# A decoder layer on one core: the convolution tiles cut into three passes, pages loaded from another queue, and three waits refilled or moved

## The chip, the cores and the metric

The kernel runs on one core of a Trainium2 chip. The metric is device time in microseconds (us), median of several runs; smaller is better. TensorE does the matrix products, VectorE (DVE in the rows), ScalarE (ACT) and GpSimd (POOL) the rest, and SyncE (SP) issues most transfers.

## The reference

One layer of inference for 256 prompt tokens and 8 sequences of 4 sample tokens, so 288 columns in all, with d_model 1024:

```
mod = silu(c) @ w_ada + b_ada            # shift1, scale1, gate1, shift2, scale2, gate2
h   = rms_norm(x) * (1 + scale1) + shift1
q, k, v, qi, ki, wi, u_conv, gates = split(h @ w_in)
A = sparse_attention(top 64 or 65 keys by the indexer, ALiBi softmax) @ w_o_attn
B = silu(layer_norm(causal_conv31(a * sigmoid(g)) + b_dw)) @ w_conv_out   # a, g = halves of u_conv
x = x + gate1 * ((sigmoid(gA) * A + sigmoid(gB) * B) @ w_out)
h2 = rms_norm(x) * (1 + scale2) + shift2
# PEER: top 16 of 16384 experts per head, gelu(u_emb . h2) * softmax gate, times v_emb
x = x + gate2 * peer(h2)
```

## The kernel before

All weights come as tiles of 128 x 1024 fp32 (512 KB) through a ring of four buffers, loaded by SP in the order of PLAN; the load of tile n waits until tile n-4 has been used. A linear tile is 8 products of 128 x 128 weights with 288 columns. It is computed in one of two ways. `linear` uses fp32 operands as they are (TensorE takes them in a slow mode). `linear_cut` cuts weights and activations into a high and a low fp32r part and makes three passes of 8 products: high x high, high x low, low x high. The high part of a tile is a copy on ScalarE (`cut_tile`), its low part a subtraction on GpSimd (`low_tile`); two cut buffers alternate. CUT lists the tiles done that way.

HEAD is the first stretch. It holds, per channel chunk k of 128, the tile conv_a k, the tile conv_g k and a part of the adaLN product (`ada`, 4 fp32 products per half, 32 columns wide); then ki, the four qi tiles, v, the k and q tiles. ScalarE applies the sigmoid to conv_g k, VectorE multiplies it with conv_a k (`gated_input`) and makes the 31-tap convolution of chunk k as 31 dependent multiply-adds of 128 x 256 on a PSUM accumulator. `settle(n)` makes VectorE wait until all but its last n recorded steps are complete; `conv_a k` for k >= 3 waits until chunk k-3 is gated. In HEAD ScalarE also issues the loads of the 16 cache pages (`load_page`), two with each conv_g tile. After the convolution VectorE does the sample tokens (a product and a reduction of 128 x 1984 for each of the four), sums the chunks for the LayerNorm, takes the reciprocal of the q/k norms, and then feeds the indexer, whose loop of 16 steps alternates on TensorE with the gate_a tiles. `L1947` is the product that spreads the q/k norms.

The second norm follows the eight out tiles: TensorE sums the squares (L1736), ScalarE and VectorE turn them into h2, and TensorE meanwhile makes one of the two last adaLN groups (`late_ada`, L1840) and then peer_q 0, with the other group between its products. After the 16 peer_q tiles the score tiles begin (128 of them, `scores`), each with a high cut on ScalarE (`cut_high`), a low cut on GpSimd (`cut_low`) and a gelu on ScalarE. At score tile 16 (SOFTMAX) ScalarE makes three exponentials for the expert gates. All engines run their own program in order, and wait on semaphores.

Of the kernel before, what the change touches and what calls it, by code (L numbers as in the profile page):

```python
# [18 lines left out]
P = 128  # L19
D = 1024  # L20
KC = D // P
# [19 lines left out]
R = 4  # L41
# [123 lines left out]
QK_AT = 3  # L165

# [10 lines left out]
def build(nc, a):  # L177
# [4 lines left out]
    with ExitStack() as ctx:  # L182
# [33 lines left out]
        class Region:  # L216
# [101 lines left out]
        windows = xn[:, :, :].rearrange("p k t -> p (k t)")[:, 0:KC * NSEQ * CW]\  # L318
            .rearrange("p (k b j) -> p k b j", b=NSEQ, j=CW)
# [77 lines left out]
        late_loaded = [sem(f"late_loaded{n}") for n in range(2 * R)]  # L397
# [43 lines left out]
        conv_in = sem("conv_in")  # L441
        vw_in = sem("vw_in")
# [93 lines left out]
        def _(sp):  # L536
            def load(n, slot):
                sp.dma_start(ring[:, slot, :], a["stream"][n]).then_inc(tile_loaded[slot], 16)

            for n, at in enumerate(LOADS):  # L540
# [5 lines left out]
                load(at, n % R)  # L546
                late = n - POS["attn_out", 2]
# [76 lines left out]
        def _(pool):  # L624
# [32 lines left out]

            for n in range(NHEAD - 2):
                low_tile(n)

# [3 lines left out]
            for n in range(NHEAD - 2, NHEAD):  # L664
                low_tile(n)
            low_tiles(("gate_a",))
# [23 lines left out]
            pool.wait_ge(tile_done, NRING)  # L690
# [10 lines left out]
            for n in range(R):  # L701
                cut_low(n, n, u_done, n - 1 if n >= 2 else None)
# [36 lines left out]
        def _(eng):  # L739
# [25 lines left out]
            for dst, src in ((staged_s, "stateT"), (wdw, "wdw"), (cvec, "cvec"), (qkg, "qkg")):  # L765
                eng.dma_start(dst, a[src]).then_inc(conv_in, 16)
# [41 lines left out]
            def load_page(n):  # L808
                page = eng.value_load(pages[0:1, n:n + 1], min_val=0, max_val=a["cache_k"].shape[0] - 1)
                for dst, src in ((cache_i[0:ID, n], "cache_i"), (cache_i[ID:P, n], "cache_i"),  # L810
                                 (cache_k[:, n].rearrange("p v n -> p (v n)"), "cache_k"), (cache_v[:, n], "cache_v")):
                    eng.dma_start(dst, a[src][bass.ds(page, 1)].rearrange("o p n -> (o p) n")).then_inc(cache_in, 16)

            for key in HEAD:
# [15 lines left out]
                elif kind == "conv_g":  # L830
                    eng.wait_ge(tile_done, POS[key] + 1)
                    nc.scalar.activation(sig[:, m], lin[BANK[key]][:, 0:T], ACT.Sigmoid).then_inc(sig_ready, 1)

                    eng.wait_ge(pages_in, 16)
                    for n in (2 * m, 2 * m + 1):
                        load_page(n)
# [140 lines left out]

            eng.wait_ge(stored, 16 * 4)
            for n in range(2 * PH):
                if n + 1 < 2 * PH:  # L980
                    cut_tile(("peer_q", n + 1))
                evac(("peer_q", n), qh[:, n])
# [21 lines left out]
            def cut_high(c, n, loaded, first=False):  # L1004

                eng.wait_ge(tile_loaded[slot_of(n)], loaded)
                if not first:

                    eng.wait_ge(hi_used, c - 1)
                    eng.wait_ge(lo_ready, c - 1)  # L1010
                nc.scalar.activation(split[:, n % 2, 0], ring[:, slot_of(n), :], ACT.Copy).then_inc(hi_ready, 1)  # L1011

# [8 lines left out]
            def first_of(n):  # L1021
                return 16 * (loads_before(n) + 1)


            eng.wait_ge(x_stored, 16)
            eng.wait_ge(tile_done, NRING)
            cut_high(0, 0, first_of(0), True)
# [4 lines left out]
            def turn(g, tokens4):  # L1032

                for n in range(R):
# [5 lines left out]
                    nc.scalar.activation(act[:, n % 2], ps[n % 2][:, 0:T], ACT.Gelu_apprx_tanh).then_inc(gelued, 1)  # L1040
                    if tokens4:
# [5 lines left out]

            with eng.Fori(1, SOFTMAX // R) as g:
# [42 lines left out]
        def _(dve):  # L1091
# [63 lines left out]
            dve.wait_ge(conv_in, 64)  # L1155
            dve.wait_ge(state_in, 1)
            dve.wait_ge(zeroed, 6)
            def gated_input(pair):
                for k in (2 * pair, 2 * pair + 1):
# [8 lines left out]
            gated_input(0)  # L1168
            for pair in range(KC // 2):
                dve.wait_ge(z_ready, 4 * pair + 4)  # L1170
                if pair:
                    dve.wait_ge(y_prompt, 2 * pair)
                for j in range(CW):
                    if j == (CW // 2 if pair == 0 else CW // 4) and pair + 1 < KC // 2:
                        gated_input(pair + 1)
                    for k in (2 * pair, 2 * pair + 1):
# [3 lines left out]
                        else:  # L1180

                            settle(1 if j < CW - 1 or k % 2 == 0 else 0)
# [7 lines left out]

            samples = y[:, :, TP:T].rearrange("p k (b t) -> p k b t", t=TD)
            dve.wait_ge(y_prompt, KC)
            step(V.tensor_copy(wdw_ps, wdw))
# [536 lines left out]
        def _(pe):  # L1730
# [7 lines left out]

            def linear(key, rhs, chunk_ready=None):

                if key[0] == "conv_a":
                    bank = pa[key[1] % 3]
                    if key[1] >= 3:

# [581 lines left out]
```

## Time and profile before

| what | value |
|---|---|
| median of 3 runs | 1259.42 us (1259.25 to 1259.59) |
| profiled execution, own time | 1258.07 us |
| its span | 1256.2 us |
| PE busy | 1213.9 us, 97% |
| DVE busy | 923.6 us, 74% |
| ACT busy | 584.4 us, 47% |
| POOL busy | 571.7 us, 46% |
| mean DMA rate | 217 GB/s |

The span is the stretch from the first to the last instruction of the profiled execution; its own time is 1.9 us longer. The busy shares are means over stages with different limits. Times in rows are counted from the start of the span.

### The profile page before, as it was taken

The numbers are of one execution on the slowest core, as the hardware profiler recorded it, in microseconds if no ns is written. First come the engines' busy times: TensorE is split into PE (matmuls) and PEld (weight loads), VectorE is DVE, ScalarE is ACT, GpSimd is POOL, SyncE is SP. The second block draws the span as 40 slices with busy tenths as digits, with TensorE's granted clock in tenths as the row PEclk, the third lists the DMA queues.
The fourth block names the chain that finished last, engine by engine and source line by source line (L and its number), as shares of the span: only waits on it lengthen the run. The fifth ranks groups of instructions, "written<-read, shape, count | busy, mean of one in ns | idle before, by whom it ended". The sixth has DMA issues, their size and how long they took to land.

```text
span 1256.2 us, 27868 instructions
## 1 busy us (share of the span) xinstructions
PE 1213.9 (97%) x8703; PEld 1110.1 (88%) x8703; DVE 923.6 (74%) x2247; ACT 584.4 (47%) x1005; POOL 571.7 (46%) x286
## 2 busy tenths in 40 slices
PE   5999999989989999999999999999999999999997
PEld 3777887989979999999999999999888888888886
DVE  4499985966754999959999999000467888888866
ACT  2202355657533445545555555444445554555453
POOL 0203454521755566766666666777303334343100
PEclk9999999999989999999999999999999999999999
DMA  9876465423743355665555555667767898888863
GB/s 361 312 266 209 150 225 188 141 85 123 264 143 123 130 185 192 203 204 176 188 178 185 179 185 179 211 210 233 252 239 272 311 342 295 312 304 307 276 230 128
DMA packets 113996, 273.11 MB, mean 217 GB/s; under 512 B 30929, under 2 KB 54193, under 8 KB 113553
## 3 DMA queue, kind: packets, MB, share of 16 engines
q1 hardware_dynamic: 98752, 243.71, 56.6%
q0 software_dynamic: 6432, 19.71, 4.6%
q10 hardware_dynamic: 8752, 8.93, 2.1%
q8 instruction: 33, 0.54, 0.2%
q14 instruction: 27, 0.21, 0.1%
HBM read 249.30 MB, written 23.00 MB: 217 GB/s over the span
## 4 chain that ended last, share of the span: by engine, by line
PE 90%; DVE 2%; DMA 2%; issue 2%; POOL 1%; ACT 1%; SPq 1%; ACTq 0%; DVEq 0%; POOLq 0%
PE ps L2185 19%; PE ps L2135 10%; PE ps L2128 10%; PE ps L2129 10%; PE ps L2188 10%; PE ps L1797 6%; PE ps L1813 6%; PE ps L1807 5%; PE ps L1755 5%; PE ps L2164 2%; DMA ring<-in_stream 1%; PE ps L1829 1%; POOL split L698 1%; PE ps L1901 1%; PE ps L2105 1%
## 5 line engine op out<-in xcount | busy, mean ns | idle before, releaser
L698 POOL TENSOR_TENSOR split<-ring,split 128x1024 fp32r<-128x1024 f32 x128 | 307.2, 2402 | 142.8 <-ACT split L1011 140.2
L1011 ACT ACTIVATE split<-ring 128x1024 fp32r<-128x1024 f32 x256 | 271.5, 1061 | 175.6 <-PE ps L2185 167.1
L2128 PE MATMUL ps<-h2r,split 128*128 128x288 f32 x1024 | 278.8, 297 | 3.2 <-ACT split L1011 3.1
L2129 PE MATMUL ps<-h2r,split 128*128 128x288 f32 x1024 | 279.0, 296 | 0.0
L2185 PE MATMUL ps<-h2r,split 128*128 128x512 f32 x1024 | 257.4, 392 | 1.4 <-DVE h2r L1644 1.4
L649 POOL TENSOR_TENSOR split<-ring,split 128x1024 fp32r<-128x1024 f32 x62 | 151.9, 2452 | 234.0 <-ACT split L796 228.0
L2185 PEld LDWEIGHTS ps<-h2r,split 128*128 128x128 f32 x1024 | 184.2, 189 | 34.5 <-ACT act L1040 1.6
L2128 PEld LDWEIGHTS ps<-h2r,split 128*128 128x128 f32 x1024 | 192.9, 188 | 3.9 <-issue 2.1
L2129 PEld LDWEIGHTS ps<-h2r,split 128*128 128x128 f32 x1024 | 192.6, 188 | 0.0
L2135 PE MATMUL ps<-h2r,split 128*128 128x288 f32 x1024 | 156.9, 295 | 0.3
L1650 DVE TENSOR_TENSOR split<-ring,split 128x1024 fp32r<-128x1024 f32 x128 | 156.0, 1218 | 0.0
L1040 ACT ACTIVATE act<-ps 128x288 f32<-128x288 f32 x124 | 51.0, 412 | 213.2 <-PE ps L2135 209.2
L2188 PEld LDWEIGHTS ps<-h2r,split 128*128 128x128 f32 x1024 | 140.1, 190 | 9.9
L2188 PE MATMUL ps<-h2r,split 128*128 128x256 f32 x1024 | 143.8, 282 | 0.0
L2135 PEld LDWEIGHTS ps<-h2r,split 128*128 128x128 f32 x1024 | 141.4, 188 | 1.5 <-POOL split L698 1.5
L711 POOL DMA_INDIRECT big<-in_stream,pick_at x32 | 58.2, 1820 | 180.1 <-DVE big L1664 132.7
L1603 DVE SCALAR_TENSOR_TENSOR hot<-ps,parts 128x256 fp32r<-128x256 f32 x256 | 124.0, 484 | 0.0
L1602 DVE TENSOR_SCALAR hot<-ps,parts 128x128 fp32r<-128x128 f32 x256 | 89.8, 351 | 11.2 <-PE ps L2164 11.2
L1183 DVE SCALAR_TENSOR_TENSOR ps<-big,ps 128x256 f32<-128x256 f32 x232 | 91.5, 480 | 0.0
L1638 DVE TENSOR_TENSOR parts<-parts,big 128x256 f32<-128x256 f32 x64 | 27.1, 424 | 82.0 <-DMA parts<-act_dram 82.0
L796 ACT ACTIVATE split<-ring 128x1024 fp32r<-128x1024 f32 x70 | 73.8, 1055 | 25.0 <-DMA ring<-in_stream 14.3
L1797 PE MATMUL ps<-h2r,split 128*128 128x288 f32 x432 | 73.0, 309 | 5.4 <-issue 2.7
(286 smaller groups left out, 1687.4 us busy)
## 6 DMA issues: line engine op xcount, KB each, us to landing
ring<-in_stream SPq DMA_DIRECT2D x371, 512.0 KB, 3.5
act_dram<-act SPq DMA_DIRECT2D x128, 128.0 KB, 1.7
big<-in_stream SPq DMA_DIRECT2D x20, 512.0 KB, 7.4
parts<-act_dram SPq DMA_DIRECT2D x16, 512.0 KB, 4.7
big<-act_dram SPq DMA_DIRECT2D x16, 512.0 KB, 5.6
big<-in_cache_k ACTq DMA_DIRECT2D x16, 128.0 KB, 3.4
big<-in_cache_v ACTq DMA_DIRECT2D x16, 128.0 KB, 3.3
s_act_dram<-act SPq DMA_DIRECT2D x128, 16.0 KB, 1.5
```

Source lines behind the costliest of these rows:

```text
L649: nc.gpsimd.tensor_tensor(split[:, n % 2, 1], ring[:, POS[CUT[n]] % R, :], split[:, n % 2, 0].bitcast(f32), ALU.subtract).then_inc(lin_lo, 1)
L698: nc.gpsimd.tensor_tensor(split[:, n % 2, 1], ring[:, slot_of(n), :], split[:, n % 2, 0].bitcast(f32), ALU.subtract).then_inc(lo_ready, 1)
L1011: nc.scalar.activation(split[:, n % 2, 0], ring[:, slot_of(n), :], ACT.Copy).then_inc(hi_ready, 1)
L1183: ins = V.scalar_tensor_tensor(acc if j < CW - 1 else y[:, k, 0:TP], zp[:, k, j:j + TP], w, acc, ALU.mult, ALU.add)
L1603: return V.scalar_tensor_tensor(hot1[:, slot], iota_ps.unsqueeze(1).to_broadcast([P, 2, P]), parts[:, 0, col], parts[:, 2:4, col].to_broad ...
L1650: V.tensor_tensor(split[:, n % 2, 1], ring[:, slot_of(n), :], split[:, n % 2, 0].bitcast(f32), ALU.subtract).then_inc(lo_ready, 1)
L1797: MM(out, hi[:, k], rhs_h[:, k], start=(k == 0), stop=False)
L2128: MM(out, u_hi[:, k], h_hi[:, k], start=(k == 0), stop=False)
L2129: last = MM(out, u_hi[:, k], h_lo[:, k], start=False, stop=False)
L2135: last = MM(out, u_lo[:, k], h_hi[:, k], start=False, stop=(k == KC - 1))
L2185: return MM(ps[k][:, 0:2 * TP], v[0][:, k], w_both, start=first, stop=last)
L2188: return MM(ps[k][:, 0:TP], v[1][:, k], wr[:, n % 2, 0], start=False, stop=False)
```

## The change

The front. The convolution tiles, but for chunk 0, join CUT. The pages are issued by SP, one behind each second tile load from position 20 on. VectorE takes the convolution chunks as 0, (1, 2), (3, 4), (5, 6), 7 and waits for the taps only, which are now loaded before the convolution state. The sum of the prompt's chunks goes to GpSimd, and the bias of the sample tokens becomes a 32nd element of the reduced window.

The back. TensorE makes products that nobody reads (`keep_busy`) at the second norm, 6 and then 2 behind each `late_ada`. The first score tile is cut before the last peer_q tile is evacuated. The exponentials stand behind the first gelu of a turn of four that is written out, outside the loop.

```diff
-STAGES = [("qi", "k", "q", "gate_a", "gate_b"), ("conv_out",), ("attn_out",), ("out",), ("peer_q",)]
-CUT = [key for key in PLAN if any(key[0] in kinds for kinds in STAGES)]
+STAGES = [("conv_a", "conv_g", "qi", "k", "q", "gate_a", "gate_b"), ("conv_out",), ("attn_out",), ("out",), ("peer_q",)]
+CUT = [key for key in PLAN if any(key[0] in kinds for kinds in STAGES) and key not in (("conv_a", 0), ("conv_g", 0))]
+GROUPS = [(0,)] + [(k, k + 1) for k in range(1, KC - 1, 2)] + [(KC - 1,)]
+PAGE_POS = NFIRST * R + R
...
                 load(at, n % R)
+                page, odd = divmod(n - PAGE_POS, 2)
+                if 0 <= page < NSEQ * NPAGES and not odd:
+                    sp.wait_ge(pages_in, 16)
+                    load_page(page)
...
+            def add_chunk(k):
+
+                pool.wait_ge(y_prompt, k + 1)
+                if k > 1:
+                    pool.wait_ge(prompt_sum, k - 1)
+                nc.gpsimd.tensor_tensor(over_y[:, 0:TP], y[:, 0, 0:TP] if k == 1 else over_y[:, 0:TP], y[:, k, 0:TP], ALU.add)\
+                    .then_inc(prompt_sum, 1)
+
             for n in range(NHEAD - 2):
                 low_tile(n)
+                for k in {15: (1, 2), 20: (3, 4), 25: (5, 6)}.get(n, ()):
+                    add_chunk(k)
...
-            pool.wait_ge(tile_done, NRING)
+            pool.wait_ge(tile_done, NRING - 1)
...
-            eng.wait_ge(conv_in, 64)
-            nc.scalar.activation(zs[:, :, :, 0:LEFT], staged_s, ACT.Copy).then_inc(state_in, 1)
+            nc.scalar.activation(warm, eps, ACT.Sigmoid)
...
-            gated_input(0)
-            for pair in range(KC // 2):
-                dve.wait_ge(z_ready, 4 * pair + 4)
-                if pair:
-                    dve.wait_ge(y_prompt, 2 * pair)
+            gated_input(GROUPS[0])
+            for g, group in enumerate(GROUPS):
+                dve.wait_ge(z_ready, 2 * group[-1] + 2)
+                if g:
+
+                    dve.wait_ge(y_prompt, group[0])
                 for j in range(CW):
-                    if j == (CW // 2 if pair == 0 else CW // 4) and pair + 1 < KC // 2:
-                        gated_input(pair + 1)
-                    for k in (2 * pair, 2 * pair + 1):
+                    if j == (CW - 1 if g == 0 else CW // 4) and g + 1 < len(GROUPS):
+                        gated_input(GROUPS[g + 1])
+                    for i, k in enumerate(group):
...
-                            settle(1 if j < CW - 1 or k % 2 == 0 else 0)
+                            settle(len(group) - 1 if j < CW - 1 or i == 0 else 0)
...
+            def keep_busy(n):
+
+                for _ in range(n):
+                    MM(pa[3][:, 0:T], g_lo[:, 0, 0:P], g_lo[:, 0], start=True, stop=True)
+
+            keep_busy(6)
             pe.wait_ge(chunk_sums, 4)
             pe.wait_ge(squares2, KC)
             sums(y[:, 0], y[:, KC - 1])
@@
             for s in range(R):
                 for j in range(2):
                     late_ada(0, s, j)
+                    keep_busy(2)
...
             with eng.Fori(1, SOFTMAX // R) as g:
                 turn(g, False)
-
-            for t in range(NT):
-                eng.wait_ge(top_max, t + 1)
-                nc.scalar.activation(tv[:, t, 0:HEADS[t]], tv[:, t, 0:HEADS[t]], ACT.Exp).then_inc(top_exp, 1)
-            with eng.Fori(SOFTMAX // R, TURN // R) as g:
+            turn(SOFTMAX // R, False, exponentials)
+            with eng.Fori(SOFTMAX // R + 1, TURN // R) as g:
                 turn(g, False)
```

On ScalarE, the front of HEAD of the kernel before: the state copy (L806), the sigmoid of conv_g (L832) and the page loads (L809, L812) between the sigmoids.

```order
L801 ACTIVATE h2r<-big 128x288 x8
L806 ACTIVATE big<-big 128x64x30
L832 ACT_TABLE_LOAD
L832 ACTIVATE big<-ps 128x288
L809 TENSOR_LOAD pages
L809 ISA x2
L812 ISA
L812 DMA big<-in_cache_i 64x128 x2
```

The same place of the changed kernel, where L837 is the warm-up sigmoid, L857 the sigmoid of conv_g and L828 the high cut of a tile.

```order
L833 ACTIVATE h2r<-big 128x288 x8
L837 ACT_TABLE_LOAD
L837 ACTIVATE big<-big 128x1
L828 ACTIVATE split<-ring 128x1024
L857 ACTIVATE big<-ps 128x288
L828 ACTIVATE split<-ring 128x1024 x2
L857 ACTIVATE big<-ps 128x288
```

The state copy and the pages are gone from here, and two cuts now stand ahead of each sigmoid: the second of them is the cut of the next chunk's conv_a tile.

On TensorE, the second norm of the kernel before: the sum of squares (L1736), the late adaLN group (L1840) and the start of peer_q 0 (L1797).

```order
L1736 MATMUL ps<-big,ones 128x288 x2
L1840 MATMUL ps<-big 32x128 x32
L1797 MATMUL ps<-h2r,split 128x288
L1840 MATMUL ps<-big 32x128 x4
L1797 MATMUL ps<-h2r,split 128x288
```

The same place of the changed kernel, where L2120 are the products that nobody reads, L1770 the sum of squares and L1875 the adaLN group.

```order
L2120 MATMUL ps<-y_r 128x288 x6
L1770 MATMUL ps<-big,ones 128x288 x2
L1875 MATMUL ps<-big 32x128 x4
L2120 MATMUL ps<-y_r 128x288 x2
L1875 MATMUL ps<-big 32x128 x4
L2120 MATMUL ps<-y_r 128x288 x2
```

The group of 32 products is now broken into 8 pieces of 4, each followed by 2 of the new products, 22 of them in all with the first 6.

On ScalarE, the exponentials (L1053) of the kernel before, and the loop of score tiles behind them with its cuts (L1011) and gelus (L1040).

```order
L1053 ACT_TABLE_LOAD
L1053 ACTIVATE big<-big 128x128 x2
L1053 ACTIVATE big<-big 128x32
L1054 UNCONDITIONAL_BRANCH
L1054 ISA
L1009 REGISTER_ALU
L1011 ACT_TABLE_LOAD
L1011 ACTIVATE split<-ring 128x1024
L1037 REGISTER_ALU
L1039 REGISTER_ALU
L1040 ACT_TABLE_LOAD
L1040 ACTIVATE act<-ps 128x288
```

The same place of the changed kernel, where L1009 is the cut, L1065 the gelu and L1078 the exponentials.

```order
L1009 ACTIVATE split<-ring 128x1024
L1065 ACTIVATE act<-ps 128x288
L1078 ACT_TABLE_LOAD
L1078 ACTIVATE big<-big 128x128 x2
L1078 ACTIVATE big<-big 128x32
L1009 ACTIVATE split<-ring 128x1024
L1065 ACT_TABLE_LOAD
L1065 ACTIVATE act<-ps 128x288
L1009 ACTIVATE split<-ring 128x1024
```

The exponentials stand one cut and one gelu later, one table load stands between them and the next gelu, and no table load stands in a loop any more; before, the loop of three turns held two.

## Rows read from the trace of the kernel before

**Rows 1.** The page's part 4, shares of the chain that ended last, by engine.

```profile
PE 90%; DVE 2%; DMA 2%; issue 2%; POOL 1%; ACT 1%; SPq 1%; ACTq 0%; DVEq 0%; POOLq 0%
```

**Rows 2.** Windows: busy us (x instructions) of PE, PEld, DVE, ACT, POOL; clock; DMA share; GB/s.

```profile
40.00:60.00 20.00, 20.00 (x109) 15.03 (x108) 10.51 (x28) 4.33 (x5) 0.00 (x0) 1.00 0.85 295
371.00:373.00 2.00, 2.00 (x19) 0.89 (x18) 2.00 (x6) 1.11 (x2) 0.81 (x1) 0.50 0.00 0
```

**Rows 3.** Timeline of TensorE in the front: start, length, instruction, [idle before].

```profile
38.48 8.03 PE L1755 MATMUL ps<-big,ring 128*128 128x288 f32 x32
...
98.31 4.15 PE L1755 MATMUL ps<-big,ring 128*128 128x288 f32 x16
...
107.58 1.32 PE L1813 MATMUL ps<-h2r,split 128*128 128x288 f32 x8
...
109.41 1.32 PE L1797 MATMUL ps<-h2r,split 128*128 128x288 f32 x8
...
112.71 1.23 PE L1797 MATMUL ps<-h2r,split 128*128 128x288 f32 x8
```

**Rows 4.** Timeline of VectorE: the convolution, the sample tokens, the q/k reciprocal.

```profile
77.28 0.99 DVE L1179 TENSOR_SCALAR ps<-big 128x256 f32<-128x256 f32 x2
...
102.73 0.99 DVE L1179 TENSOR_SCALAR ps<-big 128x256 f32<-128x256 f32 x2
...
152.70 0.42 DVE L1193 COPY ps<-big 128x248 f32<-128x248 f32 x1
153.15 2.22 DVE L1196 TENSOR_TENSOR big<-big,ps 128x1984 f32<-128x1984 f32 x1
...
179.50 1.94 DVE L1208 RECIPROCAL big<-big 10x288 f32<-10x288 f32 x1 [1.93 <-ACT big L859]
```

**Rows 5.** One line, L1183: the multiply-add of the convolution, ns min/median/max.

```profile
L1183 DVE SCALAR_TENSOR_TENSOR ps<-big,ps x232: 475/481/484, 51.4 to 151.4; 128x256 f32<-128x256 f32 x116
```

**Rows 6.** Timeline of TensorE: the product that spreads the q/k norms.

```profile
182.50 0.75 PE L1947 MATMUL ps<-big,ident 10*128 10x288 f32 x2
```

**Rows 7.** Timelines of GpSimd: low part of the activations; low part of a tile.

```profile
34.41 5.17 POOL L640 TENSOR_TENSOR h2r<-big,h2r 128x2304 fp32r<-128x2304 f32 x1 [1.87 <-ACT h2r L801]
...
110.38 2.40 POOL L649 TENSOR_TENSOR split<-ring,split 128x1024 fp32r<-128x1024 f32 x1 [0.50 <-ACT split L796]
```

**Rows 8.** Timeline of ScalarE's queue: first issues of two pages in a row.

```profile
50.52 1.14 ACTq L812 DMA_DIRECT2D big<-in_cache_i  x2
...
53.52 0.49 ACTq L812 DMA_DIRECT2D big<-in_cache_i  x1
```

**Rows 9.** DMA issues from 25 to 110 us: count, KB each, median us to landing.

```profile
ring<-in_stream SPq DMA_DIRECT2D x31, 512.0 KB, 4.9
```

**Rows 10.** Timeline of TensorE at the second norm.

```profile
363.92 1.95 PE L1840 MATMUL ps<-big 128*32 128x128 f32 x64
368.52 0.37 PE L1797 MATMUL ps<-h2r,split 128*128 128x288 f32 x1 [2.64 <-ACT h2r L975]
...
369.18 0.40 PE L1797 MATMUL ps<-h2r,split 128*128 128x288 f32 x1
...
380.18 1.47 PE L1797 MATMUL ps<-h2r,split 128*128 128x288 f32 x8
```

**Rows 11.** Timelines of TensorE and ScalarE: first score tile, and third passes of score tiles.

```profile
441.83 0.38 ACT L1000 ACTIVATE big<-ps 128x256 f32<-128x256 f32 x1
...
443.30 0.37 PE L2128 MATMUL ps<-h2r,split 128*128 128x288 f32 x1 [1.53 <-ACT split L1011]
...
445.77 1.34 PE L2135 MATMUL ps<-h2r,split 128*128 128x288 f32 x8
...
497.09 1.23 PE L2135 MATMUL ps<-h2r,split 128*128 128x288 f32 x8
...
531.88 1.23 PE L2135 MATMUL ps<-h2r,split 128*128 128x288 f32 x8
```

**Rows 12.** Timeline of ScalarE around the exponentials.

```profile
495.59 1.28 ACT L1053 ACT_TABLE_LOAD   x1
...
497.53 1.28 ACT L1011 ACT_TABLE_LOAD   x1
498.82 1.06 ACT L1011 ACTIVATE split<-ring 128x1024 fp32r<-128x1024 f32 x1
```

More of the change, by code:

```diff
@@ L396, in build @@
         wide_loaded = [sem(f"wide_loaded{n}") for n in range(NWIDE)]
-        late_loaded = [sem(f"late_loaded{n}") for n in range(2 * R)]
+        late_loaded = wide_loaded[0:2 * R]
         late_done = sem("late_done")
@@ L538, in load, with load_page @@
                 sp.dma_start(ring[:, slot, :], a["stream"][n]).then_inc(tile_loaded[slot], 16)
+            def load_page(n):
+                page = sp.value_load(pages[0:1, n:n + 1], min_val=0, max_val=a["cache_k"].shape[0] - 1)
+                for dst, src in ((cache_i[0:ID, n], "cache_i"), (cache_i[ID:P, n], "cache_i"),
+                                 (cache_k[:, n].rearrange("p v n -> p (v n)"), "cache_k"), (cache_v[:, n], "cache_v")):
+                    sp.dma_start(dst, a[src][bass.ds(page, 1)].rearrange("o p n -> (o p) n")).then_inc(cache_in, 16)
             for n, at in enumerate(LOADS):
@@ L976, in _, with cut_high, first_of @@
                     .then_inc(rhs_hi, 1)
+            def cut_high(c, n, loaded, first=False):
+                eng.wait_ge(tile_loaded[slot_of(n)], loaded)
+                if not first:
+                    eng.wait_ge(hi_used, c - 1)
+                    eng.wait_ge(lo_ready, c - 1)
+                nc.scalar.activation(split[:, n % 2, 0], ring[:, slot_of(n), :], ACT.Copy).then_inc(hi_ready, 1)
+            def first_of(n):
+                return 16 * (loads_before(n) + 1)
             eng.wait_ge(stored, 16 * 4)
@@ L981, in _ @@
                     cut_tile(("peer_q", n + 1))
+                else:
+                    eng.wait_ge(x_stored, 16)
+                    eng.wait_ge(tile_done, NRING - 1)
+                    cut_high(0, 0, first_of(0), True)
                 evac(("peer_q", n), qh[:, n])
@@ L1030, in _, with turn @@
                 gelu(c, c, c < 2)
-            def turn(g, tokens4):
+            def turn(g, tokens4, behind_first=None):
                 for n in range(R):
@@ L1040, in turn @@
                     nc.scalar.activation(act[:, n % 2], ps[n % 2][:, 0:T], ACT.Gelu_apprx_tanh).then_inc(gelued, 1)
+                    if behind_first and n == 0:
+                        behind_first()
                     if tokens4:
@@ L1153, in _, with gated_input @@
                     V.tensor_tensor(smp, smp, wide(mod[:, 0, k, 1:NG]), ALU.add).then_inc(h_ready, 1)
-            dve.wait_ge(conv_in, 64)
-            dve.wait_ge(state_in, 1)
+            dve.wait_ge(taps_in, 32)
             dve.wait_ge(zeroed, 6)
-            def gated_input(pair):
-                for k in (2 * pair, 2 * pair + 1):
+            def gated_input(group):
+                for k in group:
                     dve.wait_ge(tile_done, POS["conv_a", k] + 1)
@@ L1737, in sums, with bank_of @@
                 last.then_inc(stats, 1)
-            def linear(key, rhs, chunk_ready=None):
-                if key[0] == "conv_a":
-                    bank = pa[key[1] % 3]
-                    if key[1] >= 3:
-                        pe.wait_ge(z_ready, 2 * (key[1] - 3) + 2)
-                else:
-                    bank = lin[BANK[key]]
-                    free(BANKED.index(key))
+            def bank_of(key):
+                if key[0] != "conv_a":
+                    free(BANKED.index(key))
+                    return lin[BANK[key]]
+                if key[1] >= 3:
+                    pe.wait_ge(z_ready, 2 * (key[1] - 3) + 2)
+                return pa[key[1] % 3]
+            def linear(key, rhs, chunk_ready=None):
+                bank = bank_of(key)
                 pe.wait_ge(tile_loaded[POS[key] % R], loaded(POS[key]))
@@ L1903, in _ @@
                     last.then_inc(v_done, 1)
-                elif key[0] in ("conv_a", "conv_g", "ki"):
+                elif key not in CUT:
                     linear(key, hT, h_ready if key == ("conv_a", 0) else None)
```

63 lines of the change are left out of this document (30 added, 33 removed).

## Prediction

> **What bounds the kernel now.** I read the chain by engine first: 90% of the span is TensorE [rows 1]. So an edit counts only where it shortens what TensorE does or waits for, and I looked at four places in the timelines.
>
> In the front TensorE works without a gap on fp32 tiles. Conv_a 1 starts at 38.5 and ki at 98.3, so seven chunks take 59.8 us, 8.55 each [rows 3]. VectorE runs beside it on the convolution until 152.7 and needs its results for the q/k reciprocal, which ends at 181.44 [rows 4]; TensorE uses that at 182.50 [rows 6]. So VectorE has only 1.06 us of slack there: a front that is faster on TensorE alone gains 1.06 us, and the rest is decided by VectorE. At the second norm TensorE waits 2.64 us, and its clock is at half (0.50, the 1.2 GHz level) for the tile after it [rows 2, 10]. At the first score tile it waits 1.53 us for ScalarE's cut, and around the exponentials ten score tiles take 34.79 us [rows 11].
>
> **The front, on TensorE.** Three passes take 3.30 us with the change of mode from fp32 in front (109.41 to 112.71) [rows 3], else 3.20, since sixteen score tiles of the same 24 products take 51.32 us [rows 11]. Third pass and ada part with both mode changes take 1.83 us (107.58 to 109.41) [rows 3]; less a third of 3.20 that is 0.76. A chunk becomes 3.30 + 3.20 + 0.76 = 7.26 instead of 8.55 us. The first cut tile meets a wait: GpSimd has the low activations at 34.41 + 5.17 = 39.58, then needs 2.40 for the tile's low part [rows 7], so its third pass starts at 42.0 and it ends at 43.05, 1.2 late. Conv_g 1 ends at 46.25, the ada part at 47.0, chunk 3 at 61.5, conv_g 4 at 68.0, and ki starts near 91 to 94 instead of 98.3. TensorE itself would be 4 to 7 us early, more with the wait of the first qi tile gone.
>
> **The pages.** ScalarE needs 3.0 us for one page [rows 8]; I take the same for SP. A page stands behind tile loads 20, 22, ..., 50. Where the load behind it would have been due sooner than 3 us, it is late: that is so when the page stands behind an ada tile (loads 25, 31, 37), since the ada part takes under 1 us. Load 31 (conv_a 5) is due when ada part 27 is done, about 62, and goes at 64 to 65.5. With the 4.9 us median to landing [rows 9] that is 69 to 70.4. ScalarE cuts it (1.06 [rows 12]) before it takes the sigmoid of conv_g 4, and behind that VectorE waits.
>
> **The front, on VectorE.** Chunk 0 alone starts when its sigmoid is there, near 39, not at 50, because taps and table come earlier. Its steps depend on each other: 0.48 us [rows 5] plus the 0.03 between dependent instructions (152.70 + 0.42 to 153.15) [rows 4], so 31 x 0.51 = 15.8 us against about 12.3 per chunk in a pair. It ends at 56. Group (1, 2) stops at its eighth tap, at 61.4, for chunks 3 and 4; the sigmoid of conv_g 4 is there at 68.4 at best, 71.9 if both late loads take 4.9, and I take 70.2. So the head start of 11 us is spent in a wait of 8 to 9 us. Behind it: gating chunk 4, 0.43; 24 of 31 taps of a pair, 19.0 (a pair without gating is 24.5: 102.73 to 152.70 is 49.97, less the 25.45 of the one before it [rows 4]); group (3, 4), 25.45; (5, 6), 24.95; chunk 7 alone, 15.9. Sum 85.7, end at 155.9, which is 3.2 later than before. Then the samples: two copies 0.65, four products and four reductions of 2.25 with 0.07 for each 32nd element, 18.3; the small last sum 0.5 (estimate from the copies); the reciprocal 1.94; gaps 0.1: 21.5 [rows 4]. The reciprocal ends at 177.4 instead of 181.44, since the bias add and the chunk sum are gone. TensorE's product goes at 177.4 instead of 182.50: **gain 5.1 us**, 6.9 with the sigmoid at 68.4, 3.4 with it at 71.9. From there TensorE is busy without a gap for 20 us, so the gain is kept. GpSimd's seven small sums stand behind tiles whose chunks are done (5 and 6 at 140), and hide in its waits: without that cover they cost about 0.6 each (a quarter of 2.40 [rows 7]). The DMA share was 0.85 in this stretch [rows 2]; shorter chunks with the same bytes bring it near 1, which is why I do not take 68.4.
>
> **The second norm.** The six products take 0.8 us of a wait, free. The late group took 1.95; its 16 new products add 16 x 0.133 = 2.1 (3.20 / 24), and each of eight mode changes there and back costs what an alternation costs in peer_q 0: 0.66 a pair, of which 0.13 + 0.24 is work, so 0.29 [rows 10]. 1.95 + 2.1 + 2.3 = 6.4, so peer_q 0 starts at 370.3, 1.8 later than now. Then 8 x 0.66 + 0.1 + 2.13 = 7.5 at full clock: 377.8 against 380.18, **gain 2.3 us**. If mode changes cost nothing the start stays and it is 4.1; if the clock falls all the same, the tile takes its 11.66 of now behind a start 1.8 later: loss 1.8. I take the full clock, since the array now works in every us but one. The Trainium skill, page "TensorE: Matmul & The Clock Gate", section "HAM oscillation — how this bites in real kernels", says that the clock falls after long idle gaps of DMA-wait kind; by it the gaps here are short, nothing would fall, and the products only cost the 1.8. The trace disagrees as far as before goes: the clock is 0.50 behind a wait of 2.64 us.
>
> **The first score tile.** Its cut is ready long before, so it starts when ScalarE's last score copy is out, at 442.2 [rows 11], not at 443.30, and its third pass no longer waits for GpSimd: 442.3 + 2.2 = 444.5 against 445.77, and the 0.1 lost in the next sixteen goes too. **Gain 1.4** (0.8 to 1.6).
>
> **The exponentials.** Ten tiles take 34.79 instead of 32.0, so 2.8 are lost, 2.1 at once and the rest to two table loads in each loop turn [rows 11, 12]. Now ScalarE loads, makes the exponentials (0.65 with gaps) and cuts tile 18: from 1.7 us after the third pass of tile 16 begins, + 1.28 + 0.65 + 1.06 = 4.7; that tile wants it at 4.27, its low part (2.40) at 6.4 and has it at 7.2. Loss 0.8; the later table load hides behind tile 18. **Gain 2.0** (to 2.5). The skill's page "ScalarE: Activation LUTs", section "What ACT_TABLE_LOAD costs", counts a drain of 1.38 us with each load. By it this gain would be near 0. The row disagrees: the cut starts 0.01 us after the load ends [rows 12].
>
> **Sum.** 5.1 + 2.3 + 1.4 + 2.0 = 10.8. Against its own 1258.07 that is 1247.3; the median of the runs is 1.35 higher, so I forecast **1248.6 us**. A difference of 0.2% (2.5 us) is about what can be told from none.
>
> **Rivals.** (a) The new products do not hold the clock (the fall only comes later, in the alternating tile, where the array works 0.37 of 0.66 us): -1.8 for +2.3, 1252.7. For: that alternation did not bring the clock back before. Chance 0.20. (b) VectorE starts late behind starved loads: sigmoid of conv_g 4 at 75 or more, the front gains nothing, 1253.7. For: the DMA share; against: 4.9 was measured with two queues at work. 0.15. (c) A chunk alone costs no more per tap than one in a pair (0.39): chunk 7 takes 3.6 less, 1245.0. Against: row and gap. 0.10. (d) The exponentials gain nothing, by the page's rule of the table load: 1250.6. 0.07. (e) Slower: the pages on SP hold up every load behind them by their full 3.0 us, six of them before conv_a 5. The front turns into a loss when that sigmoid comes after 75.3, and the whole change when it comes after 81; six full delays put it at 86, 5 us slower, 1264. Against: only three of eight chunks have a load due within 3 us of a page. 0.03. My forecast keeps 0.45, within 1246.5 to 1251.
>
> The range takes in (a), (b) and (c): 1244.5 to 1254. Faster 0.95, same 0.02, slower 0.03.
>
> **What would show it.** After: the chunk's pitch on TensorE 7.3 with small waits before conv_a 3, 5, 7; VectorE idle 8 to 9 us in group (1, 2), ended by ScalarE's sigmoid; convolution end near 156; the norms' product near 177.4; clock 1.00 through peer_q 0; score tile 0's third pass 1.3 us closer to the last copy; one late tile, 18, at the exponentials. I am wrong if VectorE does not wait in group (1, 2), if chunk 7's taps are not 0.51 apart, or if the clock falls in peer_q 0.

## The result and the profile after

The changed kernel takes 1250.15 us (median of six) against 1259.34 for the kernel before (1257.89 to 1262.15). One of the six was disturbed (2364.41 us); the other five took 1248.21 to 1250.94, with a median of 1249.61, and the ratio, 0.9919 with a 95% interval of 0.9905 to 0.9932, is taken without it. The forecast was 1248.6, in a range of 1244.5 to 1254.0. The profiled execution took 1250.70 us, 7.4 less than that of before, so the two traces hold 7.4 of the 10.2 us that the ratio gives.

The page's part 4 after the change, shares of the chain by engine. TensorE had 90% of it [rows 1]:

```profile
PE 82%; DVE 10%; DMA 2%; issue 1%; SPq 1%; ACT 1%; POOL 1%; ACTq 0%; DVEq 0%; POOLq 0%
```

VectorE now holds 10%: the front's convolution sets when the q/k reciprocal is done, and TensorE waits for it. Timeline of TensorE in the front, as [rows 3, 6]:

```profile
41.64 1.34 PE L1848 MATMUL ps<-h2r,split 128*128 128x288 f32 x8 [1.01 <-POOL split L668]
47.44 1.32 PE L1832 MATMUL ps<-h2r,split 128*128 128x288 f32 x8 [0.48 <-ACT split L828]
...
71.21 1.30 PE L1832 MATMUL ps<-h2r,split 128*128 128x288 f32 x8 [0.78 <-ACT split L828]
...
94.59 4.15 PE L1791 MATMUL ps<-big,ring 128*128 128x288 f32 x16
...
179.61 0.75 PE L1983 MATMUL ps<-big,ident 10*128 10x288 f32 x2 [1.45 <-DVE big L1242]
180.28 1.43 PE L1832 MATMUL ps<-h2r,split 128*128 128x288 f32 x8
181.51 2.12 PE L1842 MATMUL ps<-h2r,split 128*128 128x288 f32 x8
183.43 1.82 PE L1848 MATMUL ps<-h2r,split 128*128 128x288 f32 x8
185.18 0.64 PE L1864 MATMUL ps<-ring,big 128*32 128x128 f32 x16
```

ki starts at 94.59 and not at 98.31, so TensorE alone is 3.7 us early, but the norm product goes 2.9 us early, behind a wait of 1.45 for the reciprocal. The tile behind that wait takes 4.90 us (180.28 to 185.18) where three passes take 3.20 to 3.30. The windows show why: the clock (third number from the end) is at its lower level.

```profile
180.00:182.00 2.00, 2.00 (x13) 1.72 (x12) 2.00 (x1) 0.00 (x0) 1.93 (x1) 0.83 0.54 217
182.00:184.00 2.00, 2.00 (x10) 2.00 (x10) 1.69 (x6) 1.46 (x3) 0.00 (x0) 0.50 0.00 0
```

Timeline of VectorE, as [rows 4]; L1190 is the gating, L1224 the new bias copy, L1242 the reciprocal:

```profile
38.27 0.43 DVE L1190 TENSOR_TENSOR big<-ps,big 128x256 f32<-128x256 f32 x1 [5.27 <-ACT big L857]
...
71.47 0.42 DVE L1190 TENSOR_TENSOR big<-ps,big 128x256 f32<-128x256 f32 x1 [7.75 <-ACT big L857]
...
141.96 15.19 DVE L1212 SCALAR_TENSOR_TENSOR ps<-big,ps 128x256 f32<-128x256 f32 x29
...
157.80 0.62 DVE L1224 COPY big<-big 128x64 f32<-128x64 f32 x1
158.29 0.43 DVE L1225 COPY ps<-big 128x248 f32<-128x248 f32 x1
...
177.62 1.93 DVE L1242 RECIPROCAL big<-big 10x288 f32<-10x288 f32 x1
```

The head start of chunk 0 goes into one wait of 7.75 us in group (1, 2), for the sigmoid of conv_g 4. ScalarE has that sigmoid at 70.98, behind a cut for which it waited on the tile load:

```profile
70.01 1.06 ACT L828 ACTIVATE split<-ring 128x1024 fp32r<-128x1024 f32 x1 [4.10 <-DMA ring<-in_stream]
70.98 0.39 ACT L857 ACTIVATE big<-ps 128x288 f32<-128x288 f32 x1
```

SyncE issued that load behind a page. The page took it 2.27 us, and the load, due when the ada part behind chunk 3 was done on TensorE at 62.98, went 2.8 us late:

```profile
63.54 1.12 SPq L553 DMA_DIRECT2D big<-in_cache_i  x2
...
65.81 1.22 SPq L547 DMA_DIRECT2D ring<-in_stream  x2
```

The second norm, as [rows 10], and its window, as [rows 2]:

```profile
361.95 1.21 PE L1770 MATMUL ps<-big,ones 128*128 128x288 f32 x4 [0.69 <-DVE big L1492]
...
369.53 0.30 PE L1832 MATMUL ps<-h2r,split 128*128 128x288 f32 x1
...
377.13 1.23 PE L1832 MATMUL ps<-h2r,split 128*128 128x288 f32 x8
```

```profile
371.00:373.00 2.00, 2.00 (x28) 0.99 (x27) 2.00 (x6) 0.28 (x1) 1.64 (x1) 1.00 0.00 0
```

The wait of 2.64 us is gone and the clock is 1.00. First score tile and exponentials, as [rows 11]: tile 18 alone is late, 3.91 us behind tile 17, not 3.20.

```profile
439.04 0.37 PE L2171 MATMUL ps<-h2r,split 128*128 128x288 f32 x1 [0.54 <-ACT big L1035]
...
441.28 1.21 PE L2178 MATMUL ps<-h2r,split 128*128 128x288 f32 x8
...
495.66 1.23 PE L2178 MATMUL ps<-h2r,split 128*128 128x288 f32 x8
...
499.57 1.32 PE L2178 MATMUL ps<-h2r,split 128*128 128x288 f32 x8
```

Added up over stretches that both traces have: front up to the first out tile 0.8, second norm 2.5, first score tiles 1.35, exponentials 2.0, together 6.6. Another 0.7 appears in the score loop, where ScalarE in the kernel before once waited for its stores and TensorE then lost 0.57 and 0.13 us at two tiles:

```profile
873.78 0.41 ACT L1040 ACTIVATE act<-ps 128x288 f32<-128x288 f32 x1 [3.57 <-DMA s_act_dram<-act]
```

The changed kernel waits there too, once, for 2.89 us, and TensorE loses nothing. The change doesn't touch that place, and I count it as chance.

### The profile page after: what moved, and what is told of

Read it like the earlier page. It is cut to its first block, busy times and chain, and to the rows that moved or that the text cites. A ratio compares the mean times of both kernels' runs of the same rounds, so it can differ in the third digit from the quotient of the medians.

```text
span 1248.9 us, 28196 instructions
## 1 busy us (share of the span) xinstructions
PE 1207.5 (97%) x8837; PEld 1114.8 (89%) x8837; DVE 921.9 (74%) x2247; ACT 592.2 (47%) x1015; POOL 616.6 (49%) x307
## 4 chain that ended last, share of the span: by engine, by line
PE 82%; DVE 10%; DMA 2%; issue 1%; SPq 1%; ACT 1%; POOL 1%; ACTq 0%; DVEq 0%; POOLq 0%
PE ps L2228 19%; PE ps L2171 11%; PE ps L2178 11%; PE ps L2172 11%; PE ps L2231 10%; DVE ps L1212 6%; PE ps L1832 5%; PE ps L1848 5%; PE ps L1842 5%; PE ps L2207 2%; DMA ring<-in_stream 2%; DVE big L1231 1%; DVE big L1228 1%; PE ps L2148 1%; SPq L557 1%
## 5 line engine op out<-in xcount | busy, mean ns | idle before, releaser
L728 POOL TENSOR_TENSOR split<-ring,split 128x1024 fp32r<-128x1024 f32 x128 | 307.4, 2402 | 138.6 <-ACT split L1009 138.6
L1009 ACT ACTIVATE split<-ring 128x1024 fp32r<-128x1024 f32 x256 | 271.6, 1061 | 174.5 <-PE ps L2228 171.5
L668 POOL TENSOR_TENSOR split<-ring,split 128x1024 fp32r<-128x1024 f32 x76 | 186.8, 2463 | 190.5 <-ACT split L828 190.5
L2171 PE MATMUL ps<-h2r,split 128*128 128x288 f32 x1024 | 278.7, 297 | 0.7 <-ACT big L1035 0.5
L2172 PE MATMUL ps<-h2r,split 128*128 128x288 f32 x1024 | 279.0, 296 | 0.0
L2228 PEld LDWEIGHTS ps<-h2r,split 128*128 128x128 f32 x1024 | 184.2, 189 | 34.5 <-issue 1.6
L2171 PEld LDWEIGHTS ps<-h2r,split 128*128 128x128 f32 x1024 | 192.9, 188 | 1.2 <-ACT big L1035 0.8
L2172 PEld LDWEIGHTS ps<-h2r,split 128*128 128x128 f32 x1024 | 192.4, 188 | 0.0
L2178 PE MATMUL ps<-h2r,split 128*128 128x288 f32 x1024 | 156.5, 295 | 0.0
L1065 ACT ACTIVATE act<-ps 128x288 f32<-128x288 f32 x124 | 51.0, 412 | 219.4 <-PE ps L2178 216.5
L741 POOL DMA_INDIRECT big<-in_stream,pick_at x32 | 62.8, 1962 | 175.6 <-DVE big L1698 127.9
L2231 PEld LDWEIGHTS ps<-h2r,split 128*128 128x128 f32 x1024 | 140.0, 190 | 9.9
L2178 PEld LDWEIGHTS ps<-h2r,split 128*128 128x128 f32 x1024 | 141.4, 188 | 0.3 <-POOL split L728 0.3
L828 ACT ACTIVATE split<-ring 128x1024 fp32r<-128x1024 f32 x84 | 88.6, 1055 | 62.9 <-DMA ring<-in_stream 52.0
L1212 DVE SCALAR_TENSOR_TENSOR ps<-big,ps 128x256 f32<-128x256 f32 x232 | 97.1, 485 | 2.0
L1832 PE MATMUL ps<-h2r,split 128*128 128x288 f32 x544 | 89.8, 306 | 3.8 <-ACT split L828 3.7
L1832 PEld LDWEIGHTS ps<-h2r,split 128*128 128x128 f32 x544 | 76.5, 190 | 14.7 <-issue 9.7
```

The costliest lines, as they stand in the source:

```text
L668: nc.gpsimd.tensor_tensor(split[:, n % 2, 1], ring[:, POS[CUT[n]] % R, :], split[:, n % 2, 0].bitcast(f32), ALU.subtract).then_inc(lin_lo, 1)
L728: nc.gpsimd.tensor_tensor(split[:, n % 2, 1], ring[:, slot_of(n), :], split[:, n % 2, 0].bitcast(f32), ALU.subtract).then_inc(lo_ready, 1)
L1212: ins = V.scalar_tensor_tensor(acc if j < CW - 1 else y[:, k, 0:TP], zp[:, k, j:j + TP], w, acc, ALU.mult, ALU.add)
L1832: MM(out, hi[:, k], rhs_h[:, k], start=(k == 0), stop=False)
L2171: MM(out, u_hi[:, k], h_hi[:, k], start=(k == 0), stop=False)
L2172: last = MM(out, u_hi[:, k], h_lo[:, k], start=False, stop=False)
```

## The experiments

All ratios are to the kernel before, timed on the same chip in the same hour, with 95% intervals. The gain in us is one less the ratio, times 1259.3. The second to fifth rows were timed together, then the sixth to ninth, then the next three, and the last alone. The median of the kernel before was 1259.34 to 1262.42 us in these five sessions, so kernels of different sessions are compared by their ratios, and a difference of such medians is only a rough one.

| kernel | median | ratio | gain |
|---|---|---|---|
| the change | 1250.15 | 0.9919 (0.9905, 0.9932) | 10.2 |
| front only | 1256.35 | 0.9965 (0.9947, 0.9983) | 4.4 |
| back only | 1255.28 | 0.9958 (0.9942, 0.9975) | 5.3 |
| no fillers | 1252.46 | 0.9932 (0.9909, 0.9954) | 8.6 |
| exponentials back | 1252.92 | 0.9938 (0.9915, 0.9960) | 7.8 |
| gating at tap 18 | 1248.39 | 0.9905 (0.9884, 0.9926) | 12.0 |
| pages late | 1252.98 | 0.9944 (0.9925, 0.9964) | 7.1 |
| pages on ScalarE | 1286.41 | 1.0202 (1.0179, 1.0225) | -25.4 |
| gating and pages | 1244.26 | 0.9878 (0.9856, 0.9901) | 15.4 |
| pages late, filled | 1249.62 | 0.9899 (0.9880, 0.9917) | 12.7 |
| one filler | 1244.39 | 0.9866 (0.9850, 0.9883) | 16.9 |
| more fillers | 1251.54 | 0.9910 (0.9891, 0.9929) | 11.3 |
| fillers in the first adaLN | 1244.39 | 0.9859 (0.9843, 0.9876) | 17.8 |

**Front only.** The changed kernel with `keep_busy`, the early `cut_high(0)` with its waits, and `exponentials()` put back as they were.

> The changed kernel with its three edits behind the front undone (the filler products at the second norm, the early cut of the first score tile, the place of the exponentials); only the rebuilt front is left. Theory A (ledger of the two traces: the q/k norm product comes 2.9 us earlier, the tile behind it runs in part at half clock and gives back 1.5, and 0.84 us is left at the second norm): 0.8 to 1.5 us faster than before, 1258.1 to 1258.5, VectorE idle 7 to 8 us in group (1, 2), and the clock at half for 3 to 4 us behind the norm product. Rival B (the recorded forecast's front term): 5.1 us, 1254.2, norm product near 177.4 and no fall of the clock. Rival C (what the medians leave when 5.4 is taken for the back): 3.7 us, 1255.6.

The gain is 4.4 us (2.1 to 6.7), above A and between C and B. The trace shows A's wait (7.66 us in group (1, 2)) and the norm product at 181.11, but behind a wait of only 0.76, and no fall of the clock there. So A's chain was right for one execution and wrong as a rule: whether the clock falls at 180 differs from trace to trace.

**Back only.** The kernel before with those three edits.

> The kernel before with the three edits behind the front alone. Theory A: second norm 2.2, first score tile 1.2, exponentials 2.0, sum 5.4: 1253.9. Rival B (the front is worth 5.1 and the rest of 9.2 is here): 4.1 us, 1255.2. Rival D (the filler products only hold the clock when the front has shifted the work before them): 1256.1, with peer_q 0 at a clock of 0.50 in part.

5.3 us (3.2 to 7.3), and by stretches of its trace 2.6 at the second norm, 1.35 at the score start and 2.0 at the exponentials: theory A. The clock is 1.00 in peer_q 0, so rival D is out. Front and back add up: 4.4 + 5.3 = 9.7 against 10.2.

**No fillers.**

```diff
-            keep_busy(6)
...
-                    keep_busy(2)
```

> The changed kernel without its 22 filler products at the second norm. Theory A (the products hold the clock, and that is worth 2.2 us net): 2.2 us slower than the changed kernel, 1252.3; peer_q 0 starts 1.8 us earlier, runs at a granted clock of 0.50 and ends 2.2 us later. Rival (the clock would stay up without them, since only the wait of 2.6 us in front mattered little): 1.8 us faster, 1248.4.

2.3 us slower by the medians, 1.6 by the ratios, whose intervals overlap; the trace decides. Its rows at the second norm:

```profile
369.14 0.37 PE L1832 MATMUL ps<-h2r,split 128*128 128x288 f32 x1 [2.65 <-ACT h2r L999]
```

```profile
372.00:374.00 2.00, 2.00 (x18) 0.77 (x18) 2.00 (x6) 0.73 (x1) 1.19 (x1) 0.50 0.02 4
```

The wait is back, the clock is at half, and the stretch from the first out tile to the products behind peer_q's first four tiles takes 54.96 us, not 52.55: the fillers are worth 2.4. They were taken out all at once, so what the 6 and what the 16 do is not told apart.

**Exponentials back.** `exponentials()` again between two loops.

> The changed kernel with the exponentials put back between two loops, one cut and one gelu earlier, two table loads in each loop turn again. Theory A: 2.0 us slower than the changed kernel, 1252.1, a wait of 1.6 us on TensorE before one score tile and 0.7 us in three small ones. Rival (by the Trainium skill, page ScalarE: Activation LUTs, section What ACT_TABLE_LOAD costs, each load drains 1.38 us wherever it stands, so the place is worth nothing): 1250.2.

2.8 us slower by the medians, 2.4 by the ratios, again with overlapping intervals. Its trace decides for A: TensorE waits 1.61 us before one score tile, and the ten tiles that took 34.79 us before take 35.05, against 32.83 with the change. In the trace of the change the gelu, the table load and the exponentials stand end to end on ScalarE, with 0.01 us between load and work (the gelu ends at 494.15):

```profile
494.16 1.28 ACT L1078 ACT_TABLE_LOAD   x1
495.45 0.63 ACT L1078 ACTIVATE big<-big 128x128 f32<-128x128 f32 x3
```

**Gating at tap 18.**

```diff
-                    if j == (CW - 1 if g == 0 else CW // 4) and g + 1 < len(GROUPS):
+                    if j == (CW - 1 if g == 0 else 18 if g == 1 else CW // 4) and g + 1 < len(GROUPS):
```

> The changed kernel with one number changed: in group (1, 2) VectorE gates the next two chunks ahead of tap 18, not ahead of tap 7. Theory A (the head start of chunk 0 is spent in the wait of 7.8 us in this group, and VectorE sets the time of the q/k norm product by 1.5 us): the wait goes, the convolution ends 7 us earlier (near 150.5), the reciprocal near 172, and TensorE takes the norm product when it gets there, near 178.2, without a wait: 1.5 us faster than the changed kernel (1248.7), 3.0 (1247.2) if the clock then never falls behind that wait. Rival (the later gating holds back TensorE's conv_a 6, which writes chunk 3's bank): no gain, 1250.2 or more, with a wait on z before conv_a 6.

1248.39, 1.8 us under the change by the medians and by the ratios, inside both intervals. The trace shows theory A's chain: the wait in group (1, 2) falls from 7.75 to 0.48 us, the convolution ends at 150.8, and the norm product goes at 179.76 without a wait. But this execution's TensorE was itself 1.7 us later in the front (ki at 96.25), so the gain shows only in the clock, 1.00 from 176 to 190.

**Pages late.**

```diff
-PAGE_POS = NFIRST * R + R
+PAGE_POS = NFIRST * R + R + 24
```

> The changed kernel with the 16 pages moved 24 loads further back in SyncE's queue, behind loads 44 to 74 instead of 20 to 50. Theory A (pages and tiles share the queue and the DMA engines, so tiles come late for the cuts: 3.7 us of waits on TensorE before conv tiles): those waits fall under 1 us in sum, ki starts 3 us earlier, the sigmoid of conv_g 4 comes near 68.5, the norm product 2 us earlier: 1248.0. Rival (it is the other transfers, v_w and the states, that take the engines): the waits stay and so does the time, 1250.2. Rival (the pages then delay the q and k tiles that follow, or the sample keys): slower, 1252.

Theory A's mechanism holds in full in the trace: no wait for a cut before a conv tile, ki at 90.44, the sigmoid of conv_g 4 at 68.40. Yet the median is 2.8 us above that of the change, and the ratio 3.1, with overlapping intervals. TensorE now waits 2.15 us for VectorE, and the clock falls behind it. The norm product's row and the window:

```profile
176.65 0.75 PE L1983 MATMUL ps<-big,ident 10*128 10x288 f32 x2 [2.15 <-DVE big L1242]
```

```profile
180.00:182.00 2.00, 2.00 (x10) 2.00 (x10) 0.00 (x0) 0.00 (x0) 1.57 (x1) 0.55 0.00 0
```

The profiled execution (1248.24, mean clock 0.995) was the fastest of six; the other five took 1251.55 to 1255.63 with 0.988 to 0.991. So what most executions lost goes with a lower clock. Where it fell in them no trace shows; the filled kernel below tests the place behind this wait.

**Pages on ScalarE.** The same page loads, two behind each sigmoid, as before the change.

> The changed kernel with the page loads put back on ScalarE, two behind each sigmoid, as before the change; all else of the rebuilt front stays. Theory A (ScalarE then has two cuts, a sigmoid and two pages of 3.0 us per chunk, 8.5 us, against 7.3 for TensorE): chunks at a pitch of 8.5 or more, the gain of the front gone, 1254 to 1256. Rival (DMA engines, not the issuing engine, bound the front): 1250.2, with the same waits before the cut tiles.

36 us over the change, where A asked for 4 to 6. ScalarE's queue, the first pair of pages of chunk 0, and TensorE:

```profile
38.71 1.21 ACTq L833 DMA_DIRECT2D big<-in_cache_i  x2
...
43.65 0.40 ACTq L833 DMA_DIRECT2D big<-in_cache_v  x1
44.42 1.06 ACT L818 ACTIVATE split<-ring 128x1024 fp32r<-128x1024 f32 x1 [6.20 <-issue]
```

```profile
57.65 1.31 PE L1832 MATMUL ps<-h2r,split 128*128 128x288 f32 x8 [3.33 <-ACT split L818]
```

Work on ScalarE does not only add up to 8.5 us per chunk, as I had put it: it stands in a circle. The cuts wait behind 6.2 us of page issues, TensorE waits for the cuts, the sigmoid waits for TensorE, and the next pages for the sigmoid. The pitch becomes 13.1 us (45.53 to 124.34 for six chunks), with the clock partly at half. So the pages' place is what makes three-pass conv tiles possible; on SyncE their cost on TensorE is the few waits of 0.5 to 1.2 us.

**Gating and pages.** Both edits.

> Both moves together, gating at tap 18 and pages 24 loads later. Theory A: VectorE is out of the way (reciprocal near 171) and TensorE arrives earlier by the waits that are gone, near 175: 4.5 us faster than the changed kernel, 1245.7. If the pages' place does nothing: as with the gating alone, 1247 to 1248.7.

1244.26: A, and 1.4 us better than said. By the ratios it is 5.2 us better than the change, and the intervals do not meet. Norm product at 174.24 without a wait; TensorE has 92% of the chain again and VectorE 2%. Each edit alone had moved the wait to the other engine.

**Pages late, filled.** Late pages, the change's gating, and 14 unread products ahead of the wait for the reciprocal.

```diff
+                    if m == 0:
+                        fill(14, pa[2])
                     pe.wait_ge(qk_rstd, 1)
```

> The kernel with the late pages (gating as in the change), plus 14 products that nobody reads ahead of TensorE's wait for the q/k reciprocal (1.9 us of work in a wait of 2.15 us). Its parent took 1248.2 to 1255.6 us in six runs, with a mean granted clock of 0.995 in the fastest and 0.988 to 0.991 in the others. Theory A (that spread and the lost gain are the clock, which falls behind this wait in most runs): mean clock 0.993 or more in most runs and a median near 1247. Rival (the clock falls elsewhere, for instance later at the small products of the sample keys): the median stays near 1253 and the clock near 0.990.

1249.62 and clocks of 0.992 in all four executions: 3.4 us better than its parent by the medians, 5.6 by the ratios, whose intervals do not meet, though not at A's 1247. That fits a clock that had fallen behind this wait, but no trace shows it held there. In the profiled execution, the slowest, the 14 fillers are followed by a wait of 6.73 us, and the clock is 0.50 from 182 to 186 all the same:

```profile
173.02 2.11 PE L1949 MATMUL ps<-h2r 128*128 128x288 f32 x14
181.87 1.32 PE L1990 MATMUL ps<-big,ident 10*128 10x288 f32 x2 [6.73 <-DVE big L1242]
```

The long wait comes from VectorE's copy, 0.23 us at its shortest, here with GpSimd beside it:

```profile
155.19 4.75 POOL L668 TENSOR_TENSOR split<-ring,split 128x1024 fp32r<-128x1024 f32 x2
...
155.96 4.76 DVE L1224 COPY big<-big 128x64 f32<-128x64 f32 x1
...
159.89 0.73 POOL L682 TENSOR_TENSOR big<-big 128x256 f32<-128x256 f32 x1
```

**One filler.** Gating and pages, and `keep_busy(1)` in place of `keep_busy(2)`.

> Both moves (gating at tap 18, late pages), with one filler product behind each four late adaLN products instead of two. Theory A (one is enough to hold the clock): 8 x 0.133 = 1.1 us less than its parent's 1244.3, so 1243.2, granted clock 1.00 from 360 to 385. Rival (one is too little): the clock is at half in the alternating tile and it is 1 to 3 us slower, 1245.5 to 1247.

The same stretch as under "no fillers" takes 51.49 us, not 52.54, at full clock:

```profile
360.00:371.00 11.00, 11.00 (x127) 7.36 (x127) 6.75 (x18) 5.80 (x14) 4.72 (x2) 1.00 0.05 9
```

That is A's 1.05 us. The medians don't show it (1244.39 against 1244.26), and the ratios, 0.9866 against 0.9878, only lean that way, with overlapping intervals.

**More fillers.** Gating and pages; `fill(5, pa[3])` before the index products of the sample keys and `fill(1, pa[3])` for every fourth of them, `fill(8, out)` before conv_out 0.

> Both moves (gating at tap 18, late pages), and filler products at two more places where the traces show a granted clock of one half behind small products or a wait: 5 ahead of the wait at the sample keys' index products and 8 among those (1.1 us of added work), and 8 ahead of the first conv_out tile (in a wait of 1.37 us). Its parent loses in its trace 3.2 of 9 us between 212 and 221 to the half clock. Theory A (the clock holds): mean clock 0.997, 1242.5. Rival (the fall there comes whatever TensorE does): 1.1 us slower than the parent, 1245.4.

4.0 us over its parent by the ratios, whose intervals just overlap; 7.2 over "one filler", timed with it, whose interval is clear of it; and 8.7 later at the first out tile than its parent in the traces (336.63 and 327.92). Not only did the clock fall there all the same, it stayed down from 217 to 231, and it fell at 206 to 212 too. Its window, TensorE busy throughout:

```profile
220.00:222.00 2.00, 2.00 (x16) 1.67 (x14) 0.00 (x0) 0.00 (x0) 0.00 (x0) 0.50 0.00 0
```

The rival is right, and its price of 1.1 us was too low. Why fillers hold the clock at the second norm and not here stays open.

**Fillers in the first adaLN.** As "one filler", and two unread fp32 products ahead of each of the five adaLN tiles before conv_a 0.

> The parent is the kernel with gating at tap 18, late pages and one filler per four adaLN products (1244.4 us). Added: two fp32 products of 128 columns that nobody reads ahead of the waits for each of the last five adaLN tiles before the first chunk (1.1 to 1.4 us apart in the traces, with waits of 0.5 to 1.6 us). In 9 of 12 traces so far the granted clock was one half from 26 to 33 us, and conv_a 0 then took 8.8 us instead of 7.94. Theory A (the clock holds): conv_a 0 at 7.9 us, first cut tile near 38.3 instead of 39.8, 1.5 us less: 1242.9. Rival (that stretch is not mended by fillers, or its gain is lost in the wait for the low parts near 42): 1244.4.

Conv_a 0 takes 7.95 us and the first cut tile starts at 38.26, as A says (8.80 and 39.81 in its parent's trace; in the other traces with the fall it took 8.9 to 9.7, but for the kernel before with 7.95). Then TensorE meets what it had outrun, GpSimd's low part and two cuts for which ScalarE waited on tile loads (5.39 and 6.64 us):

```profile
41.97 1.32 PE L1848 MATMUL ps<-h2r,split 128*128 128x288 f32 x8 [1.02 <-POOL split L668]
62.44 1.29 PE L1832 MATMUL ps<-h2r,split 128*128 128x288 f32 x8 [0.26 <-ACT split L828]
78.60 1.29 PE L1832 MATMUL ps<-h2r,split 128*128 128x288 f32 x8 [1.40 <-ACT split L828]
```

and the median is 1244.39, as the rival said. Its ratio, 0.9859, is the lowest of all, but not apart from its parent's.

## Why the prediction was right, and where not

**The direction and the place of the number.** 10.8 us were forecast; the runs give 10.2 (8.6 to 12.0), the traces 7.4. Three of four terms hold in stretches that several traces have in common. The fourth, the front, is nearly half of the sum, and there the closeness is in part luck: the chain that was to carry it gave 2.9 us in the trace and not 5.1.

**Second norm.** Forecast 2.3, with peer_q 0 at 1.8 later and full clock. Measured 2.4 to 2.6 in traces with and without the front, and 2.4 lost when the fillers are taken out. Rival (a), that they do not hold the clock, is out: 1.00 in every trace with them, 0.50 in every trace without. Even one per four small products is enough.

**First score tile.** Forecast 1.4, measured 1.35 (from the last products before the score tiles, which the score copies read, to the third pass of the third tile, 13.13 and 11.78 us).

**Exponentials.** Forecast 2.0 with one late tile and 0.8 lost. Measured 2.0 between the traces, the late tile 18 with 0.71 + 0.13 lost, 2.2 in the trace of the kernel that puts them back and 2.4 by its ratio. Rival (d) is out. The Trainium skill's page "ScalarE: Activation LUTs", section "What ACT_TABLE_LOAD costs", counts a drain of 1.38 us with a load, and here the exponential starts 0.01 us behind it.

**The front.** Here the forecast's step was mis-sized: "The reciprocal ends at 177.4 instead of 181.44". It ended at 179.55. The forecast's 70.2 is the time at which the sigmoid of conv_g 4 is there and VectorE goes on; it went on at 71.47 (the sigmoid starts at 70.98). So of the 2.1 us, 1.3 is that sigmoid, 0.5 the convolution behind it (86.2 to its end at 157.66, not 85.7; 0.4 of it in chunk 7), and 0.4 the sample part with its bias copy. The mechanism stood as told: chunk 0 alone at 0.52 us per tap (15.19 for 29) and chunk 7 too, so rival (c) is out; a wait of 7.75 us in group (1, 2); a load behind a page as its cause, though a page takes SyncE 2.3 us and not the 3.0 taken over from ScalarE. With the pages out of the way the sigmoid ended at 68.81, against 68.4 as the best case.

The second step that failed is "From there TensorE is busy without a gap for 20 us, so the gain is kept". TensorE was indeed busy without a gap, from 179.61 to 209.21, but the gain was not kept: TensorE had come to the product 1.45 us before VectorE's result, and behind that wait the tile cost 1.5 us more at half clock. The forecast had priced the clock at the second norm and left it out here.

Measured, the front is worth 4.4 us (2.1 to 6.7) in timed runs. Its traces put the norm product 2.7 us earlier in the mean (180.98 in four, 183.64 in two with the old front), and the first out tile only 1.6 (334.95 and 336.60). Forecast 5.1. Rivals (b) and (e), late sigmoid or a loss, did not occur: the sigmoid never started after 73.4 with the pages on SyncE.

**What stays open.** Which of the places gives one trace a fall of the clock and the next none. The change waited 1.45 us at the norm product and the clock fell; the kernel with the exponentials back waited 1.61 and it did not. The kernel without fillers waited 1.98 us for a cut at 73.56 and kept its clock, then 1.79 at 90.11 and lost it. Open too is why the timed runs give the front more than its traces do; and the parts of the front (the order of the chunks, the earlier taps and sigmoid table, the sum on GpSimd) were not tested one by one, only the pages and the gating were.

## What to carry to other kernels

When two engines are within 1 or 2 us of each other, an edit that speeds up one of them turns into a wait on the other: undo and redo them in pairs (by the ratios gating alone 1.8 and late pages alone a loss of 3.1, neither clear of the noise, both together a gain of 5.2). Before moving work to another queue, look at what stands in a circle with it: two pages between two cuts, chunk by chunk, cost 36 us, not their own length. And a wait on TensorE has two prices, its own length and the clock behind it; a few unread products in it, or a later consumer, are cheap tests of the second. Test each place by itself: such products gained 2.4 us at one and lost at another.

## What the hardware showed that I had not expected

**The spread between executions goes with the clock.** In 20 executions of the kernel before, the fastest (1254.28) had a mean granted clock of 0.994 and the slowest (1263 to 1264) 0.985 to 0.988; a straight line through all 20 gives 0.92 us for each 0.001 of clock, with a correlation of -0.86; the changed front alone ran from 1250.90 (0.994) to 1260.18 (0.987). In nine of the thirteen traces before the last run the clock was one half somewhere from 24 to 34 us, and in every trace at or behind the index products of the sample keys, between 212 and 232 (with the pages on ScalarE at 256 to 264), where TensorE works through small products. There the engine is not idle: busy 2.00 of 2.00 us, though in the change's trace waits of 1.38 and 0.74 us stand ahead of the fall at 222, at 209 and 217. The Trainium skill's page "TensorE: Matmul & The Clock Gate", section "HAM oscillation — how this bites in real kernels", ties the falls to long idle gaps, waits for DMA; the traces here show falls behind waits of 1.45, 1.79, 2.15 and 2.64 us, and within busy work.

**VectorE's copy waits for GpSimd.** The same 128 x 64 copy took 0.23 to 0.26 us in five traces, 0.62 to 2.44 in six and 4.76 in one. In the six it ends about 0.1 us behind the GpSimd instruction that was at work when it began. In the one it waits through three in a row, two tiles and a sum that ends at 160.62. In four of the five quick ones GpSimd computed nothing at that time, and in the fifth the copy falls where one of its sums gives way to the next. The Trainium skill's page "SBUF — State Buffer", section "SBUF: two separate sides", tells of a port pair that the two engines share and lock for a whole instruction; the traces agree, and the one with three in a row shows a wait longer than one instruction. The rebuilt front adds this copy to VectorE's path.
